# Two blocks on one core: VectorE makes the low half of each normalised tile two rounds after the tile's first instruction, instead of three

## The reference, cut to what matters

```python
x = layer_norm(DEEPNORM_ALPHA * x + jnp.einsum('bsm,md->bsd', mix, w_out[l]), ln1_g[l], ln1_b[l])
x = layer_norm(DEEPNORM_ALPHA * x + moe_ffn(x, ...), ln2_g[l], ln2_b[l])
```

```python
f = swiglu(rms_norm_2(h, g[0]), w_gate, w_up, w_down)
h = h + 0.5 * rms_norm_2(f, g[1])
```

## Time and profile before

| what | value |
|---|---|
| median of three runs | 3658.58 us (3656.79 to 3659.56) |
| the profiled execution, its own time | 3656.91 us |
| span of that execution, first to last instruction | 3654.2 us |
| mean granted TensorE clock, as a share of full speed | 0.928 |
| TensorE busy, matmuls | 3317.5 us (91%) |
| VectorE busy | 1960.0 us (54%) |
| ScalarE busy | 1401.4 us (38%) |
| GpSimd busy | 389.2 us (11%) |

### The profile page before, as it was taken

One profiled execution on the slowest core, in us unless ns is written; L12 is line 12 of the kernel. 1 busy time (PEld: TensorE's weight loads), 2 busy tenths in 40 slices (PEclk: granted clock), 3 DMA queues, 4 the chain that ended last, 5 costly groups with the idle time before them and its releaser, 6 DMA issues.

```text
span 3654.2 us, 41675 instructions
## 1 busy us (share of the span) xinstructions
PE 3317.5 (91%) x14542; PEld 2619.1 (72%) x14542; DVE 1960.0 (54%) x3050; ACT 1401.4 (38%) x2056; POOL 389.2 (11%) x235
## 2 busy tenths in 40 slices
PE   7798889987997999899988899989998999979998
PEld 5576667765675777788866788868886767668886
DVE  4753687557536875554456543455354443455353
ACT  3443567444434675322222322233123444432221
POOL 2101022322010323100010000010001000010000
PEclk9869899988598999899999999999999999899998
DMA  3101399511012996132312232323233212013232
GB/s 114 49 1 58 108 318 326 191 58 55 1 58 73 324 322 231 55 101 89 98 59 74 69 99 90 99 79 126 91 99 117 87 35 70 24 52 95 94 95 78
DMA packets 174975, 389.50 MB, mean 107 GB/s; under 512 B 11313, under 2 KB 70065, under 8 KB 174193
## 3 DMA queue, kind: packets, MB, share of 16 engines
q1 hardware_dynamic: 173424, 377.45, 31.6%
q0 software_dynamic: 1408, 10.23, 0.8%
HBM read 381.34 MB, written 6.29 MB: 106 GB/s over the span
## 4 chain that ended last, share of the span: by engine, by line
PE 69%; DVE 13%; DMA 8%; ACT 5%; DVEq 3%; issue 2%; POOL 0%; ACTq 0%; SPq 0%; POOLq 0%
PE ps L530 18%; PE ps L532 18%; PE ps L531 18%; DMA gate_up_stage<-in_w_gu 7%; PE ps L619 4%; DVE moe_lo L1683 4%; PE ps L641 3%; PE ps L625 2%; PE ps L721 2%; ACT moe_hi L982 2%; PE ps L789 1%; PE ps L684 1%; PE ps L609 1%; PE ps L592 1%; DVE tmp L1882 1%
## 5 line engine op out<-in xcount | busy, mean ns | idle before, releaser
L530 PE MATMUL ps<-xs_hi,w_hi 128*128 128x512 f32 (+2 forms) x2032 | 819.0, 403 | 101.6 <-DVE xs_lo L1417 53.4
L1361 DVE TENSOR_TENSOR w_lo<-w_stage,w_hi 128x1024 fp32r<-128x1024 f32 (+3 forms) x328 | 423.1, 1291 | 886.2 <-ACT w_hi L982 884.8
L532 PE MATMUL ps<-xs_hi,w_lo 128*128 128x512 f32 (+2 forms) x2032 | 809.9, 399 | 0.0
L531 PE MATMUL ps<-xs_lo,w_hi 128*128 128x512 f32 (+2 forms) x2032 | 809.4, 398 | 0.0
L982 ACT ACTIVATE w_hi<-w_stage 128x1024 fp32r<-128x1024 f32 (+3 forms) x360 | 392.7, 1092 | 1045.2 <-PE ps L532 1033.4
L530 PEld LDWEIGHTS ps<-xs_hi,w_hi 128*128 128x128 f32 (+2 forms) x2032 | 388.7, 191 | 211.6 <-issue 85.1
L532 PEld LDWEIGHTS ps<-xs_hi,w_lo 128*128 128x128 f32 (+2 forms) x2032 | 387.8, 191 | 89.9
L531 PEld LDWEIGHTS ps<-xs_lo,w_hi 128*128 128x128 f32 (+2 forms) x2032 | 389.2, 192 | 86.4
L1683 DVE TENSOR_TENSOR moe_lo<-gate_up_stage,moe_hi 128x1024 fp32r<-128x1024 f32 x224 | 268.5, 1242 | 115.3 <-ACT moe_hi L982 115.0
L982 ACT ACTIVATE moe_hi<-gate_up_stage 128x1024 fp32r<-128x1024 f32 x224 | 226.4, 1054 | 137.8 <-DMA gate_up_stage<-in_w_gu 133.5
L532 PE MATMUL ps<-h_hi,w_lo 128*128 128x512 f32 x704 | 278.3, 395 | 0.0
(11 more groups left out here) (333 smaller groups left out, 4817.8 us busy)
## 6 DMA issues: line engine op xcount, KB each, us to landing
gate_up_stage<-in_w_gu SPq DMA_DIRECT2D x112, 1024.0 KB, 5.5
w_stage<-in_f_gu SPq DMA_DIRECT2D x174, 512.0 KB, 3.6
down_stage<-in_w_dn SPq DMA_DIRECT2D x112, 512.0 KB, 5.8
w_stage<-in_f_dn SPq DMA_DIRECT2D x64, 704.0 KB, 4.0
w_stage<-in_w_in SPq DMA_DIRECT2D x30, 512.0 KB, 3.5
w_stage<-in_d_qk SPq DMA_DIRECT2D x24, 512.0 KB, 3.5
w_stage<-in_w_out SPq DMA_DIRECT2D x16, 512.0 KB, 3.5
w_stage<-in_d_v SPq DMA_DIRECT2D x12, 512.0 KB, 3.4
```

What stands on the lines that cost most here:

```text
L530: pe.matmul(o, lh, rh, start=start, stop=False)
L531: pe.matmul(o, lh, rl_, start=False, stop=False)
L532: return pe.matmul(o, ll, rh, start=False, stop=stop)
L1361: tt(w_lo[:, s, 0:n], stage[:, s, 0:n], w_hi[:, s, 0:n].bitcast(F32), ALU.subtract).then_inc(w_split, 1)
```

## The change

In both loops the low half of tile m is done in round m + 2, not in round m + 3, and both loops get one round fewer. No instruction is added or removed, except one drain for each loop; `ffn3_out` is as it was.

```diff
@@ layer_norm
-                for i in range(KD + 3):
+                for i in range(KD + 2):
                     if i < KD:
                         tt(norm_tile(i), src[:, i, :], ps[:, RB, :], ALU.mult)
                     if 1 <= i <= KD:
                         tt(norm_tile(i - 1), norm_tile(i - 1), ps[:, MB, :], ALU.add).then_inc(tile_ready, 1)
-                    if i >= 3:
-                        m = i - 3
+                    if i >= 2:
+                        m = i - 2
                         if last:
                             low_part("ffn0", m)
                         else:
@@ residual
-                for m in range(KD + (3 if after else 1)):
+                for m in range(KD + (2 if after else 1)):
                     if m < KD:
                         stt(tmp[:, m % 2, :], t[:, m, :], ngain[:, GAIN[name], m:m + 1], ps[:, RB, :], ALU.mult, ALU.mult)
                     if 1 <= m <= KD:
                         tt(x[:, m - 1, :], x[:, m - 1, :], tmp[:, (m - 1) % 2, :], ALU.add).then_inc(x_new if after else y_final, 1)
-                    if after and m >= 3:
-                        low_part(after, m - 3)
+                    if after and m >= 2:
+                        low_part(after, m - 2)
                     v.drain()
```

## The result

The changed kernel takes 3666.28 us, the median of 22 runs; the kernel before, run beside it 22 times, takes 3659.52. The ratio is 1.0016, 95% interval 1.0009 to 1.0023: slower by 3 to 8 us. One of the 22 executions of the kernel before took 4769.59 us, in a slow state, and is left out of the ratio; the median is the same without it. The forecast was 3665.2, +6.6 against the median of three runs.

A forecast was written before the change was run, and what follows sets the result against it. TensorE holds 69% of the chain and waits for VectorE's low halves, so the loops lie on the path. Norms 2.7 + 1.4 and residuals 2.5 give +6.6 us, 3665.2 against the median; range 3658 to 3676, the forecast alone 3663 to 3667.

The forecast's parts named there:

- Norms 1 to 3, +0.9 each: Layer norms 1 to 3: last low half starts 0.90 us later through ScalarE's chain; +2.7 us in all.
- Norm 4, +1.4: Layer norm 4, three ScalarE writes a tile: ScalarE now waits for VectorE's queued instructions; +1.4 us.
- Residuals, +0.5 each: Five residual loops: VectorE's waits at GpSimd's additions grow to 4.05 us, TensorE ends 0.5 later each; +2.5 us.
- The near-tie: Residuals: VectorE's tt starts 0.03 us ahead of GpSimd's addition and goes first; the next low half is held +1.03 us.
- the longer low halves lead by the same steps to +0.5: Residual before the dilated branch: low halves of 1.1 us, same pattern as the other residuals, +0.5 us.
- what the pieces do to the clock: Rival, residuals: smaller pieces leave the last three tiles at 1.2 GHz, +4.2 us a loop; 3674 or 3686, chance 0.07.
- price of 1.4 us for a tile at 1.2 GHz: TensorE's clock rival, residuals: each of a loop's last three tiles would take 1.4 us more at 1.2 GHz.
- The sum: Whole kernel: 2.7 for norms 1 to 3, 1.4 for norm 4, 2.5 for residuals; +6.6 us.
- GpSimd goes first: Rival, residuals: GpSimd's addition takes the port, each tt of rounds 3 to 7 held 1.17 us; +16.6, 3675, chance 0.18.
- the waits stay as they were: Rival, residuals: waits at GpSimd unchanged, residuals -3.3 us, norms +4.1; 3659.4 us, chance 0.20.
- the early low half pays everywhere: Rival, all nine loops: ScalarE's work is hidden, 0.7 to 1.4 us gained in each; 3646 to 3652, chance 0.08.
- The rule that issue order decides: Residuals: GpSimd and two-SBUF-input VectorE instructions exclude each other, issue order decides; VectorE's 0.03 us lead gives the same sum.

The follow-up runs named there:

- drain_before_add: Against the kernel before: residuals' low halves two rounds behind, plus a VectorE drain between stt and tt of tiles 2 to 7; norms as before. 3667.04 us, one run.
- mixed_first_early: Against the kernel before: residuals' low halves of tiles 1 to 3 three rounds behind, tiles 0 and 4 to 7 two; norms as before. 3658.59 us, one run.
- no_sums_two: Against the kernel before: residuals' low halves two rounds behind, GpSimd's additions in residuals and branches from pool on replaced by constant writes. 3642.25 us, one run.
- the mixed order: Against the kernel before: residuals' low halves three rounds behind for tiles 0 to 3, two for 4 to 7. 3655.80 us, ratio 0.9988; repeated 3655.42, 0.9987.

## Why the prediction was right

**Norms 1 to 3, +0.9 each: right.** The last low half starts 16.62 us into the loop, 15.72 before: +0.90 in each. It was 374.64 by the rows' layout, which is 16.62 from the start at 358.02. The waits came nearly as they were put: 0.21 us at tile 0, where the prediction had 0.3, and 0.72 ahead of the last low half, where it had about 0.9 (another 0.21 came one low half sooner). SyncE's queue in norm 2 moved from 16.55 to 17.44, +0.89. In the routers the step behind moved by 1.0 on average.

**Norm 4, +1.4: right.** The last low half moved by 1.43, its L592 by 23.14 - 21.71 = 1.43. ScalarE waits for VectorE at L1021 as said.

**Residuals, +0.5 each: right in four, too small in the fifth.** The tt of tile 2 was to start 5.05 us into the loop and GpSimd's addition 5.08; they did. Low half 1 was to end at 7.43 and ended at 7.42; low half 5 at 18.89 and 18.87; L592 at 23.24 and 23.24 to 23.27. The near-tie went to VectorE in all ordinary loops of the new order: their last low halves end at 21.17 to 21.21 in every profile. What the step "the longer low halves lead by the same steps to +0.5" missed is the residual after ffn2: +0.76 with the clock at 2.4 GHz, and +1.9 to +2.8 with part of it at 1.2. The prediction had asked what the pieces do to the clock only for all five loops or for two, at +4.2 each and a chance of 0.07. It came in one loop, in three profiles of four, and cost 1.1 to 2.0 us there beyond the 0.76. Its price of 1.4 us for a tile at 1.2 GHz was too high as well: a tile took 1.15 more.

**The sum.** The loops' marks give 3 x 0.9 + 1.43 + 4 x 0.53 + 2.1 (the mean of four profiles in the residual after ffn2, 26.99 - 24.93) + 2 x 0.1 (the routers) = 8.5 us, against 6.6. The two measured ratios make +5.9 and +8.8 us. So the total fits the forecast, and fits the larger sum as well; the runs are too wide apart to choose. Neither sum holds the jobs behind L592, for which the prediction took it that they only start later; they cost 2.1 and 1.2 us more in the two profiles of the changed kernel than in the one of before. That 6.6 came so near the measured total is in part luck: the terms of the loops are shown one by one, their sum in the time is not.

**The rivals.** That GpSimd goes first is ruled out by the rows, and drain_before_add shows what it would have cost. That the waits stay as they were is out too: they grew from 2.79 to 4.06. That the early low half pays everywhere is out: mixed_first_early shows that the early start is worth nothing, and no_sums_two that a gain of 0.73 a residual was there to be had, but for GpSimd. The rule that issue order decides (the Trainium skill, "SBUF — State Buffer", Who interferes with whom) held in both directions: VectorE 0.03 us ahead, VectorE kept its 0.68; GpSimd 0.13 ahead, GpSimd kept its 1.28.

## What to carry to other kernels

Ask of an instruction that is moved forward which other one it pushes back, and who waits for that; at the end of a loop only the last tiles count, so lag long where the cover is needed and short where the loop ends (in the residuals here: 4.4 and 4.8 us faster than before in 3660, where the 95% intervals of the ratio reach to 1.0000 and 0.9999). Where two engines share a port, lay both out in time to hundredths of a microsecond: which pairs meet is worth more than the place of one instruction (2.31, 2.79 or 4.06 us of waits for the same five additions). Compare profiles loop by loop and not by their spans: here two executions of one kernel differed by 17.6 us, of which the change was none.

## What the runs showed of the hardware that was not expected

- An idle of 0.47 us on VectorE that nothing explains cost 1.6 us at L592, since it changed which operations met GpSimd's, and the next residual began 6.4 us later than in the kernel before, TensorE's clock included. It came in one loop of one profile.
- A GpSimd write of a constant, 128x512, took 0.53 us and held no VectorE instruction, though it started within 0.01 us of a tt (at 1887.84 against 1887.83 in no_sums_two). The two kernels without additions were built on this; it held. Of GpSimd's two operations in these loops only the addition, which reads two tensors, held VectorE.
- In three executions of the same loop, the granted clock in the last stretch of the residual after ffn2 was 1.00, 0.59 and 0.62, and L592 moved by 2.0 us between the first and the others.
- The stretch from norm 1 to 2, of about 385 us, varied by 16 us between profiles, twice the effect studied here, and the waits for the experts' weights in it by as much (58.4 to 74.5 us).
- Whether the clock falls in the job behind L592 repeated by place from profile to profile: in the three profiles of the mixed order it took 7.0 us after pool and ffn1, and 5.9 in the three other residuals.
